# A second result buffer in the expert loop, and the last stage joined to the expert block

## The reference, cut to what matters

```
sh1, sc1, g1, sh2, sc2, g2 = modulation(c)            # from the conditioning vector; one set for the prompt, one for the sample
x = x + g1 * mixer(modulate(x, norm_mix, sh1, sc1))    # two attentions and the output projection
x = x + g2 * hier_moe(modulate(x, norm_ffn, sh2, sc2)) # 32 experts, 2 per row
y = rmsnorm(x, norm_final)
hier_moe: y = sum over the row's 2 experts of cw * (silu(h @ w_gate) * (h @ w_up)) @ w_down
```

## Time and profile before

| | |
|---|---|
| median of 3 runs | 1359.57 us |
| profiled execution | 1351.79 us, of which the span from first to last instruction is 1349.6 us |
| TensorE matmul busy | 1161.5 us (86%) |
| VectorE, ScalarE, GpSimd busy | 518.6, 342.2, 295.1 us |
| mean granted TensorE clock | 0.941 |
| HBM read and written | 196.62 and 30.03 MB |
| `mix_out` | about 695 to 922 us |
| `experts` | 922.6 to 1300.4 us |
| `finish` | 1300.4 to 1349.6 us |

### The profile page before, as it was taken

The page is one execution under the profiler, slowest core; times in us unless marked ns, Lnnn a source line. Parts: engine busy times, 40 slices in busy tenths (PEclk is TensorE's granted clock), DMA queues, the critical chain, the costliest instruction groups (busy, mean ns, idle before and its releaser), DMA issues. The chain is left out here.

```text
span 1349.6 us, 19893 instructions
## 1 busy us (share of the span) xinstructions
PE 1161.5 (86%) x7175; PEld 767.0 (57%) x7175; DVE 518.6 (38%) x1320; ACT 342.2 (25%) x854; POOL 295.1 (22%) x233
## 2 busy tenths in 40 slices
PE   4688999999999999999886999951998999899846
PEld 2346888888888888888773555521333333333312
DVE  2432244444444444535533466653112121111118
ACT  4422233333332333333442222110101011111102
POOL 2031313030302121110002565533112221211001
PEclk9677999999999999999998999975999899999978
DMA  9771202020102121110130111115998999999646
GB/s 372 291 287 50 71 19 89 1 88 3 60 11 70 53 78 45 54 53 26 47 140 8 63 53 57 47 32 236 419 393 313 386 379 388 376 374 363 249 185 250
DMA packets 53538, 218.56 MB, mean 162 GB/s; under 512 B 9904, under 2 KB 26680, under 8 KB 42560
## 3 DMA queue, kind: packets, MB, share of 16 engines
q1 hardware_dynamic: 36912, 117.26, 23.7%
q10 hardware_dynamic: 7632, 82.05, 15.3%
q0 software_dynamic: 8896, 17.93, 3.4%
HBM read 196.62 MB, written 30.03 MB: 168 GB/s over the span
## 5 line engine op out<-in xcount | busy, mean ns | idle before, releaser
L729 PE MATMUL att_piece_ps<-hT_hi,w_hi 128*128 128x384 f32 (+1 forms) x528 | 185.2, 351 | 2.0 <-DVE att_k_lo_sb L857 0.8
L1595 PE MATMUL moe_gu_ps<-moe_a_gu_sb,moe_xT_sb 128*64 x416 | 184.4, 596 | 2.0 <-DVE moe_xT_sb L1737 2.0
L1598 PE MATMUL moe_gu_ps<-moe_b_gu_sb,moe_xT_sb 128*64 128x512 f32 x416 | 184.4, 596 | 0.0
L729 PE MATMUL att_piece_ps<-hT_hi,w_lo 128*128 128x384 f32 (+1 forms) x528 | 173.6, 329 | 0.0
L729 PE MATMUL att_piece_ps<-hT_lo,w_hi 128*128 128x384 f32 (+1 forms) x528 | 173.2, 328 | 0.0
L916 DVE COPY att_pT_sb<-att_pT_ps 128x512 f32<-128x512 f32 (+2 forms) x192 | 94.6, 521 | 134.0 <-PE att_pT_ps L790 133.4
L1200 PE MATMUL mix_y_ps<-mix_w_out_sb,mix_oT_sb 128*128 128x512 f32 (+1 forms) x288 | 127.2, 600 | 2.2 <-ACT mix_oT_sb L1268 2.2
L1595 PEld LDWEIGHTS moe_gu_ps<-moe_a_gu_sb,moe_xT_sb 128*64 128x64 f32 x416 | 57.2, 138 | 121.2 <-issue 121.2
L977 ACT ACTIVATE att_probs_sb<-att_probs_sb,att_nmax_sb 128x640 f32<-128x640 f32 (+5 forms) x144 | 101.2, 703 | 42.1 <-DVE att_nmax_sb L902 41.3
L902 DVE CUSTOM_DVE_ANT_0 att_probs_sb<-att_s_ps,att_bias_sb 128x640 f32<-128x640 f32 (+5 forms) x144 | 95.2, 662 | 26.8 <-PE att_s_ps L778 14.6
L729 PEld LDWEIGHTS att_piece_ps<-hT_hi,w_hi 128*128 128x128 f32 x528 | 99.8, 189 | 9.4 <-issue 4.7
(11 more groups left out here) (280 smaller groups left out, 1801.6 us busy)
## 6 DMA issues: line engine op xcount, KB each, us to landing
moe_b_gu_sb<-in_w_gu ACTq DMA_DIRECT2D x26, 2048.0 KB
moe_b_dn_sb<-in_w_dn ACTq DMA_DIRECT2D x26, 1024.0 KB
moe_a_gu_sb<-in_w_gu SPq DMA_DIRECT2D x10, 2048.0 KB
keep_rows_all_sb<-in_w_ada SPq DMA_DIRECT2D x8, 2048.0 KB, 12.2
att_w_raw_sb<-in_w_qkv SPq DMA_DIRECT2D x21, 512.0 KB, 3.3
moe_a_dn_sb<-in_w_dn SPq DMA_DIRECT2D x10, 1024.0 KB
in_w_ada_sb<-in_w_ada SPq DMA_DIRECT2D x4, 2048.0 KB, 11.5
in_x_sb<-in_x_prompt SPq DMA_DIRECT2D x8, 512.0 KB, 7.0
```

The lines of the kernel that those rows point to most:

```text
L729: ins = pe.matmul(bank[:, 0:hi - lo], w[:, kind, kc, :], x[:, kc, lo:hi], start=(m == 0), stop=(m == 3 * NC - 1))
L1595: pe.matmul(gu_ps[p % 2][LANE[0], :], xT[:, c, LANE[0]], a_gu[:, bass.ds(slot, 1), c, :].rearrange("p a n -> p (a n)"), start=(c == 0), st ...
L1598: ins = pe.matmul(gu_ps[p % 2][LANE[1], :], xT[:, c, LANE[1]], b_gu[p % 3][:, c, :], start=(c == 0), stop=(c == NC - 1))
```

## The change

1. `y_sb` becomes two buffers, `y[p % 2]`, with a semaphore for each. y of step p waits for scatter p-2.
2. `g2` becomes a tile of `mix_out`. After the eight copies SP stores row 0 of it (prompt and sample, 8 KB) to a new DRAM tensor `gate2`, and only then begins its tiles.
3. `finish` is gone as a stage of its own. Each engine's part stands behind its loop in the Block of `experts`; there is no drain and no barrier between. `ya`, `norm` and `g2` lie in the buffer of `a_gu`, `yb` and `squares` in that of `b_gu`; the sums use three PSUM tiles, those of xT, of gate and up, and of y, in place of four. SP waits until all gate and up matmuls are done, loads `norm_final` and both rows of `gate2` (spread over the partitions), waits for the scatters of both buffers and then reads `expert_rows`. GpSimd no longer waits for the scatters.

```diff
-            g2 = c.enter_context(nc.sbuf_tensor("gate2_rows", [P, 2, D], F32))
...
+        sp.wait_ge(gate_out, 2 * len(GATES))
+        sp.dma_start(k["gate2"].rearrange("n d -> (n d)").unsqueeze(0), g2[0:1, :, :].rearrange("p n d -> p (n d)")).then_inc(g2_stored, 16)
         over_steps(sp, step)
+        sp.wait_ge(g2_stored, 16)
...
-    y = s.sb("y", [P, D])
+    y = [s.sb(f"y{j}", [P, D]) for j in range(2)]
...
+    freed = [w.rearrange("p s c n -> p (s c n)").rearrange("p (t n) -> p t n", n=D)
+             for w in (a_gu[:, :, :, :], b_gu_all[:, :, :, :])]
+    ya, norm, g2 = freed[0][:, 0:TILES, :], freed[0][:, TILES, :], freed[0][:, TILES + 1:TILES + 3, :]
+    yb, squares = freed[1][:, 0:TILES, :], freed[1][:, TILES, :]
+    sum_ps = [xT_ps[:, :, :].rearrange("p c n -> p (c n)"), gu_all_ps[:, :, :].rearrange("p c n -> p (c n)"), y_ps[:, :]]
...
+        n = look(sp, T_ROUNDS, 0, 1, ROUNDS)
+        alone(sp, gu_ready, 2 * n, waited)
+        sp.dma_start(norm, rep(a["norm_final"], 0, P)).then_inc(norm_ld, 16)
+        sp.dma_start(g2[:, 0, :], rep(k["gate2"][0], 0, P)).then_inc(gate_ld, 16)
+        sp.dma_start(g2[0:DEC, 1, :], rep(k["gate2"][1], 0, DEC)).then_inc(gate_ld, 16)
+        alone(sp, scattered[0], 16 * n, waited)
+        alone(sp, scattered[1], 16 * n, waited)
+        for t in range(TILES):
+            r = rows_of(t)
+            sp.dma_start(ya[0:r, t, :], k["yrows"][t * P:t * P + r, :]).then_inc(back[t], 16)
+            sp.dma_start(yb[0:r, t, :], k["yrows"][t * P + TOK:t * P + TOK + r, :]).then_inc(back[t], 16)
...
-                                    bounds_check=2 * TOK - 1, oob_is_err=False).then_inc(scattered, 16)
+                                    bounds_check=2 * TOK - 1, oob_is_err=False).then_inc(scattered[p % 2], 16)
...
+        pool.memset(half[:, :], -0.5).then_inc(half_set, 1)
         n = look(pool, T_ROUNDS, 0, 1, ROUNDS)
...
         in_rounds(pool, n, body)
-        alone(pool, scattered, 32 * n, waited)
...
+            pe.wait_ge(back[t], 32)
+            if t >= 3:
+                pe.wait_ge(gated, t - 2)
+            for n in range(0, D, 512):
+                pe.matmul(sum_ps[t % 3][0:r, n:n + 512], ident[0:r, 0:r], ya[0:r, t, n:n + 512], start=True, stop=False)
...
-            if p:
-                act.wait_ge(scattered, 16 * p)
-            act.activation(y[:, 0:512], y_ps[:, 0:512], ACT.Copy, scale=entry[:, p, 2:3].bitcast(F32))\
+            if p >= 2:
+                act.wait_ge(scattered[p % 2], 16 * (p // 2))
+            act.activation(y[p % 2][:, 0:512], y_ps[:, 0:512], ACT.Copy, scale=entry[:, p, 2:3].bitcast(F32))\
...
-            if p:
-                dve.wait_ge(scattered, 16 * p)
+            if p >= 2:
+                dve.wait_ge(scattered[p % 2], 16 * (p // 2))
...
+        dve.wait_ge(gate_ld, 32)
         residual(0)
         dve.wait_ge(norm_ld, 16)
```

More of the change, by code:

```diff
@@ L176, in build @@
             with ExitStack() as c2:
-                mix_out(nc, Scope(nc, c2, "mix"), a, o, k, g2)
+                mix_out(nc, Scope(nc, c2, "mix"), a, o, k)
             with ExitStack() as c2:
-                experts(nc, Scope(nc, c2, "moe"), a, k)
-            with ExitStack() as c2:
-                finish(nc, Scope(nc, c2, "fin"), a, o, k, g2)
+                experts(nc, Scope(nc, c2, "moe"), a, o, k)
 def modulation_rows(pe, w, sc, out):
@@ L1448, in experts @@
     a_gu, a_dn = s.sb("a_gu", [P, SLOTS, NC, 2 * DE]), s.sb("a_dn", [P, SLOTS, 2, D])
-    b_gu = [s.sb(f"b_gu{j}", [P, NC, 2 * DE]) for j in range(3)]
+    b_gu_all = s.sb("b_gu", [P, 3, NC, 2 * DE])
+    b_gu = [b_gu_all[:, j, :, :] for j in range(3)]
     b_dn = [s.sb(f"b_dn{j}", [P, 2, D]) for j in range(2)]
@@ L1472, in experts @@
     y_ready, y_out_act, y_out_dve = s.sem("y_ready"), s.sem("y_out_act"), s.sem("y_out_dve")
+    norm_ld, gate_ld, half_set, stored = s.sem("norm_ld"), s.sem("gate_ld"), s.sem("half_set"), s.sem("stored")
+    back = [s.sem(f"back{t}") for t in range(TILES)]
+    summed, gated, x_done, sq_done, ms_done, rstd_done, out_ready = (
+        s.sem(n) for n in ("summed", "gated", "x_done", "sq_done", "ms_done", "rstd_done", "out_ready"))
     block = s.ctx.enter_context(nc.Block())
@@ L1656, in _ @@
         in_rounds(pe, look(pe, T_ROUNDS, 0, 1, ROUNDS), body)
+        for t in range(TILES):
+            r = rows_of(t)
+            pe.wait_ge(back[t], 32)
[3 more added lines that the diff above has]
+                pe.matmul(sum_ps[t % 3][0:r, n:n + 512], ident[0:r, 0:r], ya[0:r, t, n:n + 512], start=True, stop=False)
+                ins = pe.matmul(sum_ps[t % 3][0:r, n:n + 512], ident[0:r, 0:r], yb[0:r, t, n:n + 512], start=False, stop=True)
+            ins.then_inc(summed, 1)
     @block.scalar
@@ L1703, in _ @@
         in_rounds(act, n, body)
+        for t in range(TILES):
+            r = rows_of(t)
+            act.wait_ge(sq_done, t)
+            act.wait_ge(x_done, t + 1)
+            act.activation(squares[0:r, :], ya[0:r, t, :], ACT.Square, accum_out=ms[0:r, t:t + 1]).then_inc(sq_done, 1)
     @block.vector
@@ L1761, in _ @@
         in_rounds(dve, look(dve, T_ROUNDS, 0, 1, ROUNDS), body)
[L1764 to L1827, removed]
```

44 lines of the change are left out of this document (31 added, 13 removed).

## The result

| | kernel before | changed kernel |
|---|---|---|
| median of the timed runs, us | 1360.72 (1359.1 to 1361.89, 4 runs) | 1329.37 (1328.19 to 1332.19, 4 runs) |
| profiled execution, us (span) | 1351.79 (1349.6) | 1328.84 (1327.0) |
| mean granted clock | 0.941 | 0.943 |

The ratio is 0.9773 with the interval 0.9753 to 0.9794: 31 us less, where 27.5 were forecast (1332, range 1319 to 1347). The two profiled executions differ by 23 us only. Which of the two numbers is the change's is a question for the experiments.

The account below looks back on a forecast made before the run. The single result buffer, waiting for each scatter, was taken to pace the expert loop, with a drain-and-barrier chain at the end. From 1359.6 us, 21 (loop) and 6.5 (joined stage) came off: 1332.1, range 1319 to 1347 for 8 in 10.

Parts of the forecast that it names:

- The result buffer sets the pace, a second one frees it: Expert loop: the wait for the previous scatter sets 13.17 us a step; with two buffers it goes altogether.
- Its size, 21 us: Expert loop gain from the second buffer: 18 us of idle DMA share plus 3 us of cushion; bounds 8 and 32.
- upper bound of 32: Expert loop: largest gain, 32 us, if the loop reaches the floor of TensorE's own work.
- 3 us of cushion: Expert loop: 3 us gained from the gate/up buffers' lead, which need not be full at the stage's end.
- What is late next: Expert loop after the scatter wait goes: TensorE's work (270.7 us for 23 steps) or the weights (270 us at 417 GB/s).
- GpSimd's order doesn't suffer: Expert loop, GpSimd's queue: the gather for p+4 stands ahead of scatter p, whose wait for y only gets shorter.
- The joined stage, 6.5 us: Kernel's end: loads wait for scatters, not drain and barrier; 6.7 us from landing to load, less 0.2, gains 6.5.
- My own lower bound of 3.6: Kernel's end: gain only 3.6 us if TensorE's branch and code fetch make it late for the first tiles.
- weights that bind: Expert loop: TensorE waits for weights every second step; loop gains 8 us, end 6.5, total 1345; chance 0.18.
- a floor reached with a warm end: Loop reaches TensorE's floor, clock stays up at the end: gains 32 + 6.5 + up to 2.6, 1319 us; chance 0.12.
- the loop that isn't freed: Expert loop: scatters queue one deeper, pace stays at 13.17 us, only the end is won: 1353 us; chance 0.04.
- the slower kernel: Expert loop: weight waits with a falling clock, 6.5 us per event; ten events give 1386 us; chance 0.05.

Follow-up runs that it names:

- drain back: Changed kernel with GpSimd draining after the last scatter's landing and the last stage's loads waiting for that drain: 1334.12 us, ratio 0.9810.
- drain aside: Changed kernel with GpSimd draining once its last scatter has landed, nobody waiting for that drain: 1326.75 us, ratio 0.9758.

## Why the prediction was right

**The result buffer sets the pace, a second one frees it.** Right. The waits for expert_rows fell from 192.2 to 8.4 us, the gate tile's from 24.8 to 1.5, the clock rose to 0.99. y to y was to be 12.1 to 12.5 us; 23 steps took 277.8 us (972.42 to 1250.25), 12.08 each as a mean. But no loop runs at 12.1: eighteen of these steps take 11.7 us and five up to 15.3. The share of the DMA engines, which I wanted at 0.97 or more, came to 0.96.

**Its size, 21 us.** The term that was mis-sized. The loop became 28 us shorter, near the upper bound of 32; with 3.6 us of the end that makes 31.6, and the timed runs say 31.4 and 32.2. Two things were in the miss. The trace I worked from had the shortest loop of the three with one buffer (320.8, against 330.4 and 327.4): against that trace alone the gain is 23.5, 2.5 more than forecast. I carried the 7.8 us between profiled and timed runs over to both kernels as a constant of the measurement, but most of it was in the loop (the second trace of before is 8.4 us longer, its loop 9.6), and the change removes what makes the loop vary. And I let the idle 6% of DMA share be the measure (18 us) with 3 us of cushion; in fact the share over 960 to 1260 us only rose from 0.94 to 0.96, but the rate from 376 to 393 GB/s, 409 per full share where I had reckoned with 400.

**What is late next.** I named TensorE's floor or the weights. TensorE it is, with 8.9 us on top that come from the load on the DMA engines and 1.7 of low clock in the last step. The weights hardly show as a wait, 0.2 us; the first to be late were the gathered rows, which I had checked only for their order in the queue ("GpSimd's order doesn't suffer") and not for how long they take to land: up to 30.3 us. My sign for trouble, a landing of scatters above 22 us, did appear (25.3), with 8.4 us of waits behind it: with two buffers a scatter has two steps, 23.4 us. In the forecast's sense the floors were right: both near 268 to 270 us for 22.8 steps, and neither quite reached (22.8 steps of 12.08 us are 275). The Trainium skill (DMA: Bandwidth & Descriptors, section Issuing engines are not separate DMA queues) says that transfers from all issuing engines interleave on the same 16 DMA engines. By that rule, the runs agree: three ways of issuing GpSimd's transfers earlier moved the lateness from one to another, and 25.2 MB less removed it. That issuing earlier buys no bandwidth either is the prediction's own step and not the page's words; these runs bear it out. As the only limit the rule was too pessimistic, for the engines move more at the same busy share.

**The joined stage, 6.5 us.** The step from landing to first load is right to 0.2 us (10.0 to 3.3 us behind the issue of the scatter, 6.7 us). The term is too large all the same, 3.6 us net in the trace (59.2 to 55.6). I had read the 6.4 us of drain as something that a Block's end costs, and not asked where GpSimd would do it if the Block ends later: it does it at the kernel's end, 7.05 us of which the last store hides all but 2.1. The rest, 1.1 us, is between the first load and the last store: the second load took 6.23 us to land instead of 4.84. In the nine other traces of a joined stage without the drain ahead of its loads this stretch is 45.7 to 47.5 us, against 45.9 and 46.1 in the two of before, so what part of it the join costs is not settled. My own lower bound of 3.6 was for another reason, TensorE arriving late; it waited 11.6 us for the load, so that did not happen.

**The clock at the end** stayed down as assumed (0.50 from 1275 to 1280 us), TensorE's first eight sums took 5.8 us from 1281.30, before 6.0.

**The rivals.** Both bounds' cases, weights that bind and a floor reached with a warm end, did not come, though the floor was missed by 10.6 us only; the loop that isn't freed (1353) and the slower kernel (1386) are far off. That 1332 was met so closely is in part luck: the two errors in size, 7 us too little in the loop and 2.9 too much at the end, have opposite signs, and 1332.1 was closer to 1329.4 than either term deserved. One more sign was there: I expected less than 1.5 us of difference ahead of 920 us, and GpSimd's drain at the end of `mix_out` stands at 922.0 against 919.4 before. In the fourteen traces it stands between 916.4 and 926.0, so this can't be told from spread.

## What to carry over

- A stage that waits for its own output buffer ran at another pace in each trace here; a profiled execution is one draw. Profile such a kernel twice before sizing a gain, compare it stage by stage, and don't carry a difference between profiled and timed runs over as a constant.
- When a drain or a barrier is taken out, ask where its work will be done instead, and put it where the engine idles anyway.
- Where transfers fill the engines, as here at a share of 0.96, a late transfer can be a symptom of the total. Moving its issue cured that wait and made another in three kernels; taking bytes away was the test.

## What was not expected of the hardware

- GpSimd's drain takes 6.44 us behind the loop, with all of its transfers landed, and 0.66 us the next time, little more than the 0.54 us of the instruction that still runs. It is paid once, at whichever drain comes first: ahead of the last stage (before, drain back), at the kernel's end as 7.05 us (changed), or beside the loads (drain aside). It seems to grow with the number of indirect transfers that GpSimd has issued since its last drain. In the kernel before, `mix_out` issues 18 of them and its drain takes 1.54 us with nothing running; the expert stage issues 78, and 6.44; with none, in the first and the last stage, 0.04 and 0.66. That is an estimate of 0.08 us for each ((6.436 - 1.541)/60). The 18 move a list entry a row, 52 of the 78 a row of 4 KB, so the bytes seem not to set it. No run here changes the number alone.

```profile
L176 POOLq DRAIN  x1: 1541/1541/1541, 919.4 to 919.4; - x1
L180 POOLq DRAIN  x1: 661/661/661, 1344.4 to 1344.4; - x1
```

- With the DMA engines at a share of 0.95 to 1.01, a gather of rows landed after 10.5 to 30.3 us (median 20.7), where a scatter into free engines took 3.2 us.
- The same busy share carried more with two buffers than with one over 960 to 1260 us: 393 GB/s at 0.96 against 376 at 0.94, 409 and 400 per full share. In the other traces that I worked out it is 397 and 399 with one buffer and 404 to 409 with two. Why isn't shown.
